# One tile instead of two: GpSimd folds the squares of eight norms, TensorE sums each with one product

## The reference

```python
def _rmsnorm(x, g):
    x32 = x.astype(jnp.float32)
    y = x32 * lax.rsqrt(jnp.mean(x32 * x32, axis=-1, keepdims=True) + EPS)
    return (y * g.astype(jnp.float32)).astype(x.dtype)
...
    for li in range(DEPTH):
        x = x + 0.5 * _swiglu(_rmsnorm(x, g[0]), ffn_w_in[li, 0], ffn_w_out[li, 0])
        h = _rmsnorm(x, g[1])
        ...
        x = x + 0.5 * _swiglu(_rmsnorm(x, g[2]), ffn_w_in[li, 1], ffn_w_out[li, 1])
        gate = jax.nn.sigmoid((_rmsnorm(x, g[3]) @ ple_w_gate[li]).astype(jnp.float32))
```

## Time and profile before

| what | value |
|---|---|
| median of 3 runs | 1484.36 us (1483.49 to 1493.59) |
| the profiled execution's own time | 1484.77 us |
| its span, first to last instruction | 1483.0 us |
| TensorE busy with matmuls | 1454.0 us, 98% of the span |
| VectorE busy | 1079.0 us, 73% |
| ScalarE busy | 778.6 us, 53% |
| GpSimd busy | 170.9 us, 12% |
| mean granted clock of TensorE | 0.999 of full |

### The profile page before, as it was taken

The page is one execution under the profiler, slowest core; times in us unless marked ns, Lnnn a source line. Parts: engine busy times, 40 slices in busy tenths (PEclk is TensorE's granted clock), DMA queues, the critical chain, the costliest instruction groups (busy, mean ns, idle before and its releaser), DMA issues.

```text
span 1483.0 us, 30971 instructions
## 1 busy us (share of the span) xinstructions
PE 1454.0 (98%) x12334; PEld 1404.9 (95%) x12334; DVE 1079.0 (73%) x1555; ACT 778.6 (53%) x1186; POOL 170.9 (12%) x218
## 2 busy tenths in 40 slices
PE   7999999999999999999999999999999999999998
PEld 7999999989999999999998999999998997889958
DVE  6886568987897568877667665797558868385692
ACT  6544455565554446544445664554446438454482
POOL 1101012711240110100110000211100100010000
PEclk9999999999999999999999999999999999999999
DMA  7877744225787646776556335697653853047500
GB/s 241 272 252 236 259 137 150 86 86 186 240 282 233 222 143 188 235 243 215 187 182 169 103 112 171 201 297 232 206 170 114 259 165 122 1 131 235 152 2 29
DMA packets 219100, 264.86 MB, mean 179 GB/s; under 512 B 22301, under 2 KB 196349, under 8 KB 219005
## 3 DMA queue, kind: packets, MB, share of 16 engines
q1 hardware_dynamic: 209032, 234.64, 50.5%
q0 software_dynamic: 8960, 27.37, 5.4%
q10 hardware_dynamic: 1013, 1.52, 0.3%
HBM read 262.44 MB, written 1.05 MB: 178 GB/s over the span
## 4 chain that ended last, share of the span: by engine, by line
PE 83%; DVE 11%; ACT 3%; DMA 2%; issue 1%; POOL 0%; SPq 0%; DVEq 0%; ACTq 0%
PE twin L1135 25%; PE twin L1137 24%; PE twin L1136 24%; DVE w_lo L1868 3%; PE twin L1558 1%; PE twin L1790 1%; PE twin L1752 1%; DVE hg_s L2104 1%; PE twin L1570 1%; PE twin L1572 1%; DVE hg_f L2086 1%; PE twin L1149 1%; DVE rs L1897 1%; DVE sq L2086 1%; DVE hg_f L2085 1%
## 5 line engine op out<-in xcount | busy, mean ns | idle before, releaser
L706 ACT ACTIVATE w_hi<-w_raw 128x1024 fp32r<-128x1024 f32 (+1 forms) x452 | 454.1, 1038 | 418.3 <-PE twin L1137 262.5
L1868 DVE TENSOR_TENSOR w_lo<-w_raw,w_hi 128x1024 fp32r<-128x1024 f32 (+1 forms) x452 | 547.4, 1248 | 151.5 <-ACT w_hi L706 151.1
L1135 PE MATMUL twin<-xh,w_lo 128*128 128x256 f32 x2296 | 647.4, 282 | 1.9 <-DVE xl L1874 1.0
L1136 PE MATMUL twin<-xl,w_hi 128*128 128x256 f32 x2296 | 639.1, 278 | 0.0
L1137 PE MATMUL twin<-xh,w_hi 128*128 128x256 f32 x2296 | 639.0, 278 | 0.0
L1135 PEld LDWEIGHTS twin<-xh,w_lo 128*128 128x128 f32 x2296 | 433.0, 189 | 4.6 <-issue 1.3
L1136 PEld LDWEIGHTS twin<-xl,w_hi 128*128 128x128 f32 x2296 | 434.0, 189 | 0.5 <-issue 0.2
L1137 PEld LDWEIGHTS twin<-xh,w_hi 128*128 128x128 f32 x2296 | 432.4, 188 | 0.0
L1135 PE MATMUL twin<-hh,w_lo 128*128 (+1 forms) x704 | 195.5, 278 | 0.0
L1136 PE MATMUL twin<-hl,w_hi 128*128 (+1 forms) x704 | 195.2, 277 | 0.0
L1137 PE MATMUL twin<-hh,w_hi 128*128 (+1 forms) x704 | 195.2, 277 | 0.0
(11 more groups left out here) (367 smaller groups left out, 1988.5 us busy)
## 6 DMA issues: line engine op xcount, KB each, us to landing
w_raw<-in_ffn_w_in SPq DMA_DIRECT2D x176, 512.0 KB, 4.7
w_raw<-in_ffn_w_out SPq DMA_DIRECT2D x88, 512.0 KB, 4.2
w_raw<-in_w_in SPq DMA_DIRECT2D x52, 512.0 KB, 4.7
mod_raw<-in_w_ada POOLq DMA_DIRECT2D x128, 192.0 KB, 4.5
w_raw<-in_a_w_in SPq DMA_DIRECT2D x32, 512.0 KB, 4.4
w_raw<-in_ple_w_gate SPq DMA_DIRECT2D x16, 512.0 KB, 3.9
w_raw<-in_b_w_out SPq DMA_DIRECT2D x16, 512.0 KB, 3.7
w_raw<-in_w_out SPq DMA_DIRECT2D x16, 512.0 KB, 4.5
```

What stands on the lines that cost most here:

```text
L706: A(w_hi[:, c % NSLOT, cols], w_raw[:, c % NRAW, cols], ACT.Copy).then_inc(*did(hi_ready))
L1135: mm(out, lhs[1], rhs[0], start=start, stop=False, skip_group_check=skip)
L1136: mm(out, lhs[0], rhs[1], start=False, stop=False, skip_group_check=skip)
L1868: V.tensor_tensor(w_lo[:, c % NSLOT, cols], w_raw[:, c % NRAW, cols], f32(w_hi[:, c % NSLOT, cols]), ALU.subtract).then_inc(*did(lo_ready))
```

## The change

`FOLDED` gains norm 4, `fold` gains a third add (one tile onto one), after which the fold counts as done, and `sums` takes one tile of a folded norm. `fold(4)` is put into GpSimd's queue behind `fold(3)`, ahead of `modulation(2)`.

```diff
-FOLDED = (0, 1, 2, 3, 5, 6, 7)
+FOLDED = (0, 1, 2, 3, 4, 5, 6, 7)
...
             pool.wait_ge(*did.last)
-            G.tensor_tensor(sq[:, 0:2, :], sq[:, 0:2, :], sq[:, 2:4, :], ALU.add).then_inc(*did(pool_steps, ("folded", s)))
+            G.tensor_tensor(sq[:, 0:2, :], sq[:, 0:2, :], sq[:, 2:4, :], ALU.add).then_inc(*did(pool_steps))
+            pool.wait_ge(*did.last)
+            G.tensor_tensor(sq[:, 0, :], sq[:, 0, :], sq[:, 1, :], ALU.add).then_inc(*did(pool_steps, ("folded", s)))
...
         fold(3)
+        fold(4)
         modulation(2)
...
-            tiles = 2 if s in FOLDED else KD
+            tiles = 1 if s in FOLDED else KD
```

## The result

The changed kernel took 1493.69 us (median of 20 executions), the kernel before 1485.33 us (20 beside it): a ratio of 1.0056, 95% interval 1.004 to 1.0072, so 8 us or 0.6% slower, inside the 1% that counts here as no change. The forecast was 1489.5 us, 1484 to 1494, and its own case 1487 to 1492. The profiled execution took 1497.03 us, with a span of 1495.2 (before: 1484.77 and 1483.0).

The account below looks back on a forecast made before the run. TensorE, busy 98% of the span, was taken as the bound, with GpSimd/VectorE turns and weight loads at some norms. -0.05 + 1.2 + 0 + 1.9 + 1.7 = +4.7 us on 1484.77 gave 1489.5 us, range 1484 to 1494.

Parts of the forecast that it names:

- its own case: The forecast sum, with norm 4's wait and one fall of the clock: 1487 to 1492 us, chance 0.50.
- Norm 4, the main term: At norm 4 TensorE waits for three adds that nothing hides, so the next chunk starts late: +1.9 us.
- +1.7 for the clock: After 4.7 us idle at norm 4, TensorE runs 3.4 us at half clock: +1.7 us.
- The turns: GpSimd adds and VectorE subtractions alternate by whole instructions; at norm 4 each xl takes 0.42 us between adds.
- The fall that the forecast took for its model: In the kernel before, 1.22 of 3 us busy, then granted clock 0.57 over 4 us: 3.4 us at half.
- Norms 3 and 7, +1.2: At norms 3 and 7 the third add delays subtractions 3 and 4, hence the weight load, by 0.6 us each.
- Norms 0, 1, 2, 6: One product less, 0.41 us each, against waits for the third add at norms 0 and 2: together -0.05 us.
- Norm 2's wait of 0.53: At norm 2 TensorE waits 0.53 us for the third add; less the product's 0.41, +0.12 us.
- What moves: modulation(2)'s w_ada loads, queued behind fold(4), issue at 582.8 instead of 573.03; 20 us of cover remain, price 0.
- the wait without the fall of the clock: Rival: norm 4's wait comes but the clock stays up; +3.5 us, 1488.3 us, chance 0.17.
- no turns: Rival: the third add slips in beside VectorE, or turns are hidden; 1484.4 to 1486.1 us, chance 0.11.
- more falls: Rival: half clock also at norms 5 and 7, 1.7 us each; 1491.2 to 1492.9 us, chance 0.15.

Follow-up runs that it names:

- the kernel before and its variant: Variant: the kernel before with one extra transpose behind norm 0's products in the first feed-forward; 1486.68 us, ratio 0.9981 to the kernel before.

## Why the prediction held, and where it failed

**Norm 4, the main term: right, by sizes that offset each other.** Forecast +1.9 for the wait and +1.7 for the clock; the segment has +3.57, and 3.5 to 4.3 in four other profiles (2.8 in the one where the lower level lasted 3.4 us only). The squares end near 588.70 and the chunk starts at 594.20, 5.5 us later; before it was 581.33 - 577.66 = 3.67. That is +1.8. The turns came as forecast, one xl behind each add: the adds end at 591.14, 592.56 and 593.42, the xl begun beside each at 591.43, 592.84 and 593.70, 0.28 us later every time, and the second and third add end 1.12 and 0.58 us after the xl ahead of them, their own lengths (forecast 1.15 and 0.61). The same holds to 0.01 us in all six profiles with norm 4 at one tile. What was off is the length of an xl's turn, 0.28 us for the forecast 0.42: the three adds took 4.6 us, not 5.0. VectorE waits the longer since an add is the longer turn. The rule cited from the Trainium skill ("SBUF — State Buffer", Who interferes with whom) agrees with these rows: the two contend, and the one that comes later waits for the other's whole instruction. The product started 0.15 us after the last add and ran at the lower clock, 0.63 us for the forecast 0.41, which made up the sum. The lower level lasted 6.8 us and not 3.4; what was left of it behind the start of the chunk, 4.2 us (594.20 to 598.4), costs 2.1 for the forecast 1.7. The two make 3.9; where the segment has 0.3 of it back was not traced. The fall that the forecast took for its model, near 316 to 322 us, is itself in seven of the fourteen profiles only; the one at norm 4 is in all six with one tile there.

**Norms 3 and 7, +1.2: wrong.** The third weight subtraction took 1.75 us, as forecast (1.8), and so the fourth is late. The chain of waits after (beside the earlier trace rows):

```profile
553.83 7.65 DVE w_lo L1871 x4
561.50 4.96 DMA w_raw<-in_kv_w_down
...
1124.60 7.66 DVE w_lo L1871 x4
1132.28 5.00 DMA w_raw<-in_w_in
```

7.65 for 7.12 us, +0.53 at norm 3. But the load behind it took 4.96 us where it took 6.01. That isn't chance: over the profiles that show it, norm 3's load took 5.34 to 6.01 us (four profiles) without the third add and 4.87 to 5.10 us (eight) with it. A load issued later landed as early. The failed step is to take the load's length as fixed and add the lateness of its issue: what releases TensorE is when the load's bytes arrive, and the load was not waiting for its issue alone. What else held it was not traced. The segment's rest is -0.44 to -0.70 us in eight profiles with one tile at norm 3, and 0 to -1.20 in six with two: no cost. At norm 7 the load gave back less, 4.8 for 5.1 us in the means of eight and six profiles, but there was no cost either: the rest is +0.2 to +1.0 us with one tile and 0 to +0.9 with two, about 0.4 in both means.

**Norms 0, 1, 2, 6: small, as forecast.** At norm 0 TensorE waited 0.90 us for the forecast 1.06; the segment's +0.28 stands for +0.65. The third add's 1.59 us fits the turns (forecast 1.6). Norm 6's -0.52 is the same to 0.01 in all nine profiles with one tile there (forecast -0.41). Norm 2's wait of 0.53 did not come here: TensorE reaches the product at 374.21, 6.6 us after its squares (before 5.9), so the tile was ready. In four of the other six profiles with one tile at norm 2 it waited, 0.2 to 0.9 us. Norm 1's -1.63 is not to be read: in the other one-tile profiles it runs from 0 to -2.0.

**What moves: right.** The modulation's first loads are issued at 593.37, 4.7 us after norm 4's squares end (before: 4.6 us ahead of that); their first reader starts at 616.88, so 23.5 us of cover are left, for the forecast 20.

**The sum.** Without the long step the five profiles of the changed kernel and its two variants with or without a transpose are 1.85 us above the three of the kernel before and its variant (means 1469.42 and 1467.57), where 4.7 were forecast: 1.2 too much at norms 3 and 7, the other 1.6 in small differences at the other norms, which scatter as much from profile to profile. That the time came out above the forecast and not below it is the term that was missing: the longer step of the matmuls, 117.8 ns, which the prediction put at nothing without a word. In these profiles it makes 8.4 of 10.3 us between the means; over the timed executions, where the whole difference is 7.0 ± 1.0 us, 7.0 - 1.85 leaves some 5 for it, which is a remainder and not a measurement. The range held by luck in part: the time lies above the forecast's own case, the norms cost less than forecast, and the omitted term had the sign that made up for it. Of the rivals, "the wait without the fall of the clock" and "no turns" are out by the stretches at norm 4, "more falls" is half right: the one fall lasted twice as long, and in one of the six profiles with norm 4 at one tile (the changed kernel with one transpose more) another came behind norm 5, at 800 us, where the segment has +1.5; none came at norm 7.

**Open.** What sets the step isn't settled in whole. It changes mostly where TensorE's stream of equal matmuls is interrupted, and one program goes at either in different executions. At norms 6 and 7 the number of tiles goes with the step right behind it in all fourteen profiles, which is as near to a cause as these runs come; why one product turns the step and two don't was not found. At norms 0 and 2, where most of the long step of the first profile lies, one tile goes with it more often only, and the timed runs put the whole price of these two norms at 1.6 to 4.0 us, of which 0.8 was forecast. That the long step's excess alone makes the scatter of one kernel's executions (15 us for the kernel before) was not tried.

## What to carry to other kernels

Where a product is worth 0.4 us and the fold that saves seven of them stands alone in front of a waiting TensorE, count the wait and the clock behind it, not the products: in single profiles a wait of 3.4 us cost about 1 us and kept the clock, one of 4.1 us cost 3.6 and lost it, and elsewhere 1.9 us went with a fall, so the clock is to be read over several executions. A weight load that comes later need not land later; compare its length over several profiles before adding its lateness to the path. And compare matmuls per microsecond in an untouched stretch before looking for the cause of a difference at the change itself: one profile each can differ by 8 us or more through no instruction that was edited. Then compare it right behind each edited place: there the edit can have set it.

## What the runs showed of the hardware

- TensorE, always busy and at a granted clock of 1.00, works through 128x256 matmuls at one of two steps, 113.3 or 117.8 ns (records of 276 or 281 ns), and keeps it over up to 186 us without a break; the long step makes such a stretch 4% longer. In the first profile of the changed kernel it held in the first two feed-forwards and cost 7 and 3.6 us there.
- Behind a sum of one tile (two matmul records) at norms 6 and 7 the stream went on at 117.8 ns in 9 of 9 and 8 of 8 profiles, behind one of two tiles (four records) at 113.3 ns in 5 of 5 and 6 of 6.
- GpSimd's adds and VectorE's subtractions of two SBUF tiles took turns, whole instruction by whole instruction: an xl subtraction begun beside an add ended 0.28 us after it, a weight subtraction some 1.1 us after it. Against three adds (4.6 us) four xl took 4.95 us in place of 1.68.
- The lower clock level lasted 3.4 us after some waits and 6.8 us at the one at norm 4 (in five of the six profiles with norm 4 folded to one tile, 3.4 us in the sixth).
- At norm 3 a load of weights took 0.7 us less when it was issued 0.5 us later (4.96 against 5.7 us, means over eight and four profiles).
